# Second attention with the values as weights and its output as features by tokens; a router with fewer and reordered steps

## The reference

```python
p = jax.nn.softmax(s, -1).astype(v.dtype)
p_nb = p[..., :kh * kw].reshape(B, H, GRID_W, kh, kw)
p_ctx = p[..., kh * kw:]
return (jnp.einsum('bqhij,biqjhd->bqhd', p_nb, v_nb)
        + jnp.einsum('bqhp,bphd->bqhd', p_ctx, v_ctx))
```

```python
g_sel = jnp.argmax(g_logits, -1)
e_in_group = jnp.take_along_axis(e_logits, g_sel[:, None, None], 1)[:, 0]
top_v, top_i = lax.top_k(e_in_group, TOP_K)
gates = jax.nn.softmax(top_v, -1) * p_g
```

## Time and profile before

| | us |
|---|---|
| median of three timed runs (lowest, highest) | 1438.0 (1436.76, 1440.14) |
| profiled execution, its own time | 1435.37 |
| its span | 1433.2 |
| TensorE busy / VectorE / ScalarE / GpSimd | 1091.2 / 382.4 / 183.3 / 244.7 |
| weights of the experts, six pieces of 1 MB each | 246 pieces |
| DMA, mean over the span | 272 GB/s |

### The profile page before, as it was taken

The page is one execution under the profiler, slowest core; times in us unless marked ns, Lnnn a source line. Parts: engine busy times, 40 slices in busy tenths (PEclk is TensorE's granted clock), DMA queues, the critical chain, the costliest instruction groups (busy, mean ns, idle before and its releaser), DMA issues.

```text
span 1433.2 us, 26875 instructions
## 1 busy us (share of the span) xinstructions
PE 1091.2 (76%) x9881; PEld 586.6 (41%) x9882; DVE 382.4 (27%) x917; ACT 183.3 (13%) x486; POOL 244.7 (17%) x446
## 2 busy tenths in 40 slices
PE   4899998697587777656648999999935757788781
PEld 1333345444244444323224444677433423444440
DVE  0120117767311111101043002322772101111117
ACT  0110026300000000000012001542000000000000
POOL 2000002200133333212112010000001212333330
PEclk9999997997599999978787999898957978999996
DMA  9866891118959999999975992101079999999932
GB/s 367 293 242 257 341 364 57 59 60 309 414 212 395 415 416 414 415 416 415 397 287 87 110 165 101 59 1 59 30 274 413 412 414 416 415 366 370 416 111 112
DMA packets 84900, 389.72 MB, mean 272 GB/s; under 512 B 17613, under 2 KB 18125, under 8 KB 56697
## 3 DMA queue, kind: packets, MB, share of 16 engines
q1 hardware_dynamic: 62624, 349.77, 63.0%
q0 software_dynamic: 15200, 36.74, 9.2%
q10 hardware_dynamic: 7032, 2.66, 0.7%
HBM read 379.65 MB, written 17.44 MB: 277 GB/s over the span
## 4 chain that ended last, share of the span: by engine, by line
DMA 40%; PE 35%; issue 10%; DVE 9%; ACT 2%; DVEq 1%; POOLq 1%; POOL 0%; SPq 0%; ACTq 0%; PEldq 0%
DMA ring<-in_w_down_dram 32%; PE ps L800 15%; PE ps L951 6%; DMA ybuf<-yo,idy 4%; PE ps L1040 4%; DMA ring<-in_w_ada_dram 2%; PE ps L1058 2%; PE ps L921 2%; PE ps L776 1%; PE ps L888 1%; DMA ring<-in_w_gate_dram 1%; PE ps L895 1%; POOLq L450 1%; PE ps L906 1%; DMA qkv<-ybuf 1%
## 5 line engine op out<-in xcount | busy, mean ns | idle before, releaser
L1040 PE MATMUL ps<-ring,xs 128*32 128x256 f32 x4928 | 311.1, 406 | 112.7 <-DMA ring<-in_w_up_dram 59.1
L1040 PEld LDWEIGHTS ps<-ring,xs 128*32 128x32 f32 x4928 | 183.8, 116 | 234.0 <-issue 126.2
L800 PE MATMUL ps<-ring,hT 128*128 128x512 f32 x576 | 256.3, 604 | 8.1 <-ACT hT L626 4.3
L1058 PE MATMUL ps<-ring,hm 128*32 128x256 f32 x2464 | 156.5, 394 | 32.0 <-ACT hm L734 26.0
L800 PEld LDWEIGHTS ps<-ring,hT 128*128 128x128 f32 x576 | 110.1, 193 | 153.4 <-issue 143.0
L1058 PEld LDWEIGHTS ps<-ring,hm 128*32 128x32 f32 x2464 | 72.8, 112 | 91.7 <-ACT hm L734 39.9
L1507 DVE COPY yo<-ps 128x256 f32<-128x256 f32 x73 | 31.0, 425 | 237.2 <-DMA ybuf<-yo,idy 179.6
L539 POOL DMA_INDIRECT xg<-xmod,idx x77 | 80.8, 1050 | 66.3 <-POOL idx L536 61.4
L731 ACT ACTIVATE sg<-ps 128x128 f32<-128x128 f32 x73 | 20.3, 278 | 560.0 <-PE ps L1040 553.2
L951 PE MATMUL ps<-ring,qT 128*128 128x512 f32 x192 | 84.7, 601 | 2.7 <-DVE qT L1309 1.6
L550 POOL DMA_INDIRECT ybuf<-yo,idy x73 | 75.1, 1029 | 64.4 <-POOL idy L547 62.6
(11 more groups left out here) (257 smaller groups left out, 853.0 us busy)
## 6 DMA issues: line engine op xcount, KB each, us to landing
ring<-in_w_gate_dram SPq DMA_DIRECT2D x82, 1024.0 KB
ring<-in_w_up_dram SPq DMA_DIRECT2D x82, 1024.0 KB
ring<-in_w_down_dram SPq DMA_DIRECT2D x82, 1024.0 KB
ring<-in_w_ada_dram SPq DMA_DIRECT2D x48, 1024.0 KB, 8.1
ring<-in_w_qkv_a_dram SPq DMA_DIRECT2D x12, 1024.0 KB, 5.2
ring<-in_w_qkv_b_dram SPq DMA_DIRECT2D x12, 1024.0 KB, 15.4
modb<-mdram POOLq DMA_DIRECT2D x12, 512.0 KB, 7.1
qkv<-ybuf SPq DMA_DIRECT2D x6, 1024.0 KB, 8.3
```

Source lines behind the costliest of these rows:

```text
L800: ins = mm(ps[:, 2 * t + hf, :], lhs[:, k, t * P:(t + 1) * P], raw[:, slot, kk * D + hf * 512:kk * D + (hf + 1) * 512], start=(k == 0), st ...
L1040: ins = mm(ps[j * BLK:(j + 1) * BLK, 1, 0:W].rearrange("p (a n) -> p a n", a=2), xs[:, k, :], w[:, :, at:at + FW], start=(k == 0), stop=(k ...
L1058: ins = mm(ps[j * BLK:(j + 1) * BLK, 5, 0:WD], hm[:, 2 * c + q, :], ring[:, slot + GU + c, q * D + j * WD:q * D + (j + 1) * WD], start=(c ...
```

## The change

In the second attention VectorE divides the probabilities of a unit by their sums before they are turned (`normalise`), the values become the weights and the turned probabilities the moving operand, each head of a pair fills its half of the PSUM partitions, and VectorE copies a unit's output straight to `oT` (`take_oT`). The 24 transposes and three copies are gone, and `w_o` is loaded in another order of rows.

```diff
 def transpose_prob(u):
-    pe.wait_ge(comb_done[l] if l == 0 else exp_done[l], u + 1)
+    pe.wait_ge(comb_done[l], u + 1)
 def attend(u):
     pe.wait_ge(pT_ev[l], u + 1)
-    w = P // maps
-    for h in range(maps):
-        lo = j * P + h * w
-        for i in range(nk):
-            ins = mm(tile_ps(3)[:, lo:lo + w], probT[u % 2][:, h, i * P:(i + 1) * P], values(t, i, lo, lo + w),
-                     start=(i == 0), stop=(i == nk - 1))
+    ...
+    else:
+        if u >= 2:
+            pe.wait_ge(o_ev[l], u - 1)
+        for i in range(nk):
+            for h in range(2):
+                ins = mm(ps[HD * h:HD * (h + 1), 6 + u % 2, 0:P], values(t, i, lo + HD * h, lo + HD * (h + 1)),
+                         probT[u % 2][:, h, i * P:(i + 1) * P], start=(i == 0), stop=(i == nk - 1))
     ins.then_inc(pv_done[l], 1)
-transpose_tiles(lambda t: o[:, t, :], o_rdy[l], oT_ps[l])
-pe.wait_ge(oT_rdy[l], NT)
+if l == 0:
+    transpose_tiles(lambda t: o[:, t, :], o_rdy[l], oT_ps[l])
+    pe.wait_ge(oT_rdy[l], NT)
+else:
+    pe.wait_ge(o_ev[l], UNITS)
```

On VectorE, where layer 1 had `take_o` once in four units:

```diff
+def normalise(u):
+    t, j = u // PAIRS, u % PAIRS
+    e = prob[u % 2][:, :, 0:keys[t]]
+    r = rsum[:, 2 * (u % 2):2 * (u % 2) + 2]
+    dve.wait_ge(exp_done[l], u + 1)
+    chain(v.reciprocal(r, sums[:, t % 2, :, j]))
+    v.tensor_tensor(e, e, r.unsqueeze(2).to_broadcast([P, 2, keys[t]]), ALU.mult).then_inc(comb_done[l], 1)
+def take_oT(u):
+    t, j = u // PAIRS, u % PAIRS
+    dve.wait_ge(pv_done[l], u + 1)
+    v.tensor_copy(oT[:, j, t * P:(t + 1) * P], ps[:, 6 + u % 2, 0:P]).then_inc(o_ev[l], 1)
 ...
-        elif u >= 5 and u % 4 == 1:
-            take_o((u - 5) // 4)
+        else:
+            normalise(u)
+            if u >= 2:
+                take_oT(u - 2)
```

```diff
 # POOL, behind the writes of o
+last = x[:, NT - 1, :]
+chain(pool.tensor_tensor(last, last, lnb[:, 2, :], ALU.mult))
+pool.tensor_tensor(last, last, lnb[:, 3, :], ALU.add).then_inc(x2_done, 1)
 pool.wait_ge(mod_used, l + 1)
 load_gates(l, 1)
 ...
-pool.wait_ge(tok_rdy[l], 1)
-pool.wait_ge(tab_rdy[l], 1)
-n_blk = table(pool, T_NBLK, 24, NB)
 pool.wait_ge(xmod_w[l], 16 * NT)
 pool.wait_ge(out_done, 32 * (l + 1))
+pool.wait_ge(tok_rdy[l], 1)
 ...
 gather(0)
+pool.wait_ge(tab_rdy[l], 1)
+n_blk = table(pool, T_NBLK, 24, NB)
 # TensorE
+pe.wait_ge(rt_dve[l], 1)
+for t in range(NT):
+    ins = mm(ps[0:NE, 5, 0:1], a_all[:, t, :], ones[:, 0:1], start=(t == 0), stop=(t == NT - 1))
+ins.then_inc(rt_pe[l], 1)
 pe.wait_ge(key_rdy[l], 1)
 ... # the two key products
-pe.wait_ge(rt_dve[l], 2)
 ... # twelve products with tri and ones
-for t in range(NT):
-    ins = mm(ps[0:NE, 5, 0:1], a_all[:, t, :], ones[:, 0:1], start=(t == 0), stop=(t == NT - 1))
-ins.then_inc(rt_pe[l], 1)
 waves(6, 7)
 pe.wait_ge(rt_dve[l], 3)
 ...
-pe.wait_ge(rt_dve[l], 5)
 for i in range(2 * NT):
+    pe.wait_ge(rt_dve[l], 5 + i)
     ins = mm(ps[:, 1, 0:NBX], rt[:, 2400 + i * P:2400 + (i + 1) * P], ...)
 # VectorE, first_max (low is iota - 1000)
-chain(v.tensor_scalar(tmp, tmp, -1000.0, 1000.0, ALU.mult, ALU.add))
-chain(v.tensor_tensor(tmp, tmp, iota3(n), ALU.add))
+chain(v.scalar_tensor_tensor(tmp, tmp, -1000.0, iota3(n), ALU.mult, ALU.add))
 chain(v.tensor_reduce(col(20, NT), tmp, AX, ALU.min))
-chain(v.tensor_tensor(one, iota3(n), b3(col(20, NT), n), ALU.is_equal))
+chain(v.tensor_tensor(one, low, b3(col(20, NT), n), ALU.is_equal))
 # VectorE, other groups
-for t in range(NT):
-    chain(v.tensor_tensor(e4[:, t], e4[:, t], oneg[:, t, :].unsqueeze(2)..., ALU.mult))
-    chain(v.tensor_tensor(e4[:, t], e4[:, t], pen[:, t, :].unsqueeze(2)..., ALU.add))
+chain(v.tensor_tensor(e4, e4, pen.unsqueeze(3).to_broadcast([P, NT, NG, EPG]), ALU.add))
```

## The result

The changed kernel takes 1423.7 us (median, 1420.6 to 1427.0) beside 1439.1 for the kernel before on the same chip: ratio 0.9902, 95% interval 0.9885 to 0.9920, 14 us less. The forecast was 1412.5, range 1405 to 1421: right in sign, 11 us too fast, and the measured time lies outside the range. The profiled execution takes 1422.7 us (span 1420.6, against 1433.2 before): 12.6 less where the steps add up to 25.5.

The account below looks back on a forecast made before the run. Bounds: expert weight loads (layer 0 hanging on TensorE's first block, layer 1 on its stream's start), TensorE in the second attention, VectorE in the routers. -7.8 - 14.8 - 4.9 + 2.0 = -25.5 from 1438.0 gives 1412.5 us, range 1405 to 1421.

Parts of the forecast that it names:

- last tile's scaling on GpSimd: Both routers: the last tile's two norm-weight multiplications leave VectorE, 2.6 us less there; modb's loads go later in layer 1.
- The prediction's own sign of being wrong: A second-attention unit above 4 us, or a first block in layer 0 less than 6 us sooner.
- a_all is ready 4.8 us sooner: Layer 0's router: logits 2.55 us sooner and a chain 2.27 shorter, so a_all at 349.2 in place of 354.04.
- The first block is 7.8 sooner: Layer 0, attention output to first expert block: 6.0 + 1.1 + 0.7 us sooner, -7.8 (bounds -6 to -9.5).
- stream +2.0: Layer 1: modb's later loads enter the weight stream that bounds the stage, costing 2.0 us.
- as the loads in that stage hang on TensorE, all of it moves: Layer 0's experts: the whole gain at the first block, 7.8 us, reaches the end of the stage.
- a unit 3.27: Second attention: TensorE's unit falls from 3.86 to 3.27 us; its last attend comes 14.8 sooner (bounds -6 to -17).
- the ring: Second attention: oT copy, maxima, two exps, copy of transposed probabilities and hand-overs, 3.27 us from an attend to later transposes.
- oT, w_o and fold, -4.9: Behind the second attention: transposes and copies vanish, w_o starts 0.4 behind the last attend, 4.9 us saved.
- Clock drop: Rival, chance 0.22: TensorE's wait in the second attention's tail lowers its clock, slowing tail and w_o; 1418 us.
- Halves in series: Rival, chance 0.12: the attend's two 64-column halves don't run beside each other, the unit stays at 3.85; 1421 us.
- Stream helped: Rival, chance 0.09: GpSimd is quick, layer 1's stream starts with the picks and gains 2.6, not losing 2.0; 1408 us.

Follow-up runs that it names:

- e4: The changed kernel with the last tile's scaling back on VectorE, behind a_all and the keys, where it waits for TensorE: 1413.0 us, ratio 0.9835.
- e5: e4 plus two GpSimd operations of 128x1024 on a scratch tile that nothing reads, issued behind modb's loads: 1414.7 us, ratio 0.9849.
- e2: The kernel before with only the router's edits (trimmed chain, last tile's transposes in halves, its scaling on GpSimd): 1439.8 us, ratio 1.0024.
- e11: e8 with layer 1's ln_g and ln_b loads issued by SyncE once the last expert's weights have landed: 1408.9 us, ratio 0.9798.
- e8: e4 with VectorE taking a unit's maxima ahead of the oT copy in the second attention: 1411.6 us, ratio 0.9824.
- e9: e4 without the position bias products in the second attention: 1405.4 us, ratio 0.9778.
- e7: e4 with the second attention's attend issued head by head in place of in turn: 1416.9 us, ratio 0.9869.

## Why the prediction was right or wrong

**The step that failed is the last tile's scaling on GpSimd.** It was put down as 1.23 to 2.5 us an operation (it took 2.37), as free for VectorE, and as +2.0 through modb's loads. With it out of the way (e4) the whole is 9.6 us faster by the ratios. The prediction's own sign of being wrong, a first block in layer 0 less than 6 us sooner, came up: its first product is 4.1 sooner. What the step did:
- In both layers it holds up VectorE's router chain. Layer 0, "a_all is ready 4.8 us sooner": 1.9 sooner with it, 5.1 without (e4). "The first block is 7.8 sooner": by the cut, the first product is 4.3 sooner with it, 8.7 without. Cost in layer 0 at GpSimd's first copy: 4.0 us (33.6 behind the cut against 29.6); with modb's loads issued first 3.6 (e5). The Trainium skill has the rule that I missed (SBUF — State Buffer, Who interferes with whom): VectorE's scalar operations in a two-port mode, and those with two inputs in SBUF against a GpSimd operation that reads SBUF, share a port pair with GpSimd, and whichever comes second waits for the whole of the other's instruction; a reduction never does. The traces agree: TENSOR_SCALAR (2.55, 1.99) and SCALAR_TENSOR_TENSOR (1.79 in e5, 2.28 in e2) wait, and the four TENSOR_REDUCE that fall beside one of GpSimd's operations in the changed kernel and e2 take their usual 0.14 to 0.17. Which mode a scalar operation ran in no trace shows, and GpSimd stayed out for far longer than one instruction of VectorE (6.84 us). I had cited the rule on how slow GpSimd is (the Trainium skill, GPSIMD Engine Reference, Performance versus the Vector engine: 1.96 times VectorE's time; here 2.37 against 1.23, 1.93 times) and not the one on its being in the way.
- In layer 1, "stream +2.0": 6.1. The second operation began 1.72 late, the picks came 1.4 later in place of 2.6 sooner, so both modb's loads and the weights were late: 4.5 by bytes, 4.7 at the last long wait for weights. The other 1.4 have no shown cause. The forecast's bounds were too narrow as well: its own starts for the loads, 1050.6 and 1053.1 against 1049.80, are 0.8 to 3.3 later and not 0.7 to 2.9, and by the cut they were 4.3 later. e4, with the picks 2.6 sooner and modb's loads 2.1 sooner, has layer 1 as before (346.3): the 2.1 MB of modb then fill the time up to the weights at some 300 GB/s, and bytes taken out of it help (layer 1 in e11 is 2.5 us less than in e4, 3.2 less than in e8). "All else that the router saves there is hidden behind the stream" held.

**Layer 0, "as the loads in that stage hang on TensorE, all of it moves".** Counted from the cut, of 4.3 at the first product 2.4 arrive at the end; in e4 6.4 of 8.7. The fifth expert's load, which waits for TensorE, is issued 3.3 sooner (430.00 before, 426.72 after); from there the DMA engines are full (share 1.02 in each window of 50 us from 430 to 580), and the last load is issued 2.3 sooner. Where that last 1.0 went I can't tell from scatter, which is 3.7 us in this stretch for one and the same code. The inner steps held: group 5.7 behind a_all (5.8), products 2.8, toki 1.9 behind them, GpSimd 0.2 behind toki (0.3).

**Second attention, "a unit 3.27", -14.8.** From the end of the projections (891.4, 889.05) to the last attend it is 11.5 shorter. TensorE's unit was mis-sized: 3.86 less 0.58 leaves out that attend takes 0.80, not 0.70, and that transposes and the bias's last instruction each grew 0.05 to 0.1 beside it. The thirteen intervals from unit 8 to unit 21 take 45.6 in place of 42.9, 2.7 of the 3.3 us missing; the start up to unit 8 and the tail (7.8, not 7.5) have 0.3 each. That both bounds came out at 3.3 was chance: the ring is 3.02 (e9). The wait behind normalise cost nothing.

**oT, w_o and fold, -4.9:** right in each part: w_o 0.39 behind the last attend, the norm 16.5 behind (16.15), tile 2 at 43.3 (43.3).

**The rivals.** Clock drop: TensorE stands still 1.70 us at 969.64, and the granted clock stays 1.00 there (windows 969.6 to 970.6 and 973 to 974), where 2.25 us before 978 were followed by a fall. Halves in series: refuted by the unit of 3.51 and the attend of 0.80; in e7, which issues them in series, even that order takes less than the forecast's 1.28. Stream helped: its premise failed. None was the true case, engines in each other's way; I had looked for waits by semaphore only. That e4 comes out at the forecast is partly luck: its middle is 4 us short of it, layer 0 1 short and layer 1 2 better, and by stretches it saves 21.8 and not 25.5.

## What to carry to other kernels

Before an operation moves to GpSimd "in parallel", list what VectorE runs beside it: a chain of 0.2 us operations waited here for nearly the whole of a 2.4 us one, twice, and GpSimd stood idle beside the chain. Look first for a gap on the engine that has the work (5 us of waiting for TensorE here), and count which loads the helper issues behind it. Where a stage is bound by a stream, only bytes ahead of it and its start count; a load taken out of its way needs a place where no other load waits behind it.

## What the runs showed of the hardware

- GpSimd: a two-input 128x1024 fp32 operation takes 2.37 us (VectorE 1.23); with all operands one tile 1.91.
- A small VectorE operation can last until GpSimd's two-input operation ends, with no tile shared: 2.39 and 1.79 us in e5, where the same forms take 0.22 and 0.26 alone.
- Between its two operations GpSimd stands idle as "issue", with nothing in the profile to name: 0.73 (e2), 1.72 and 2.57 us, and 6.84 in e5. That it waits for VectorE's chain is inferred; the same code gave 0.73 in one execution and 2.57 in another.
- A VectorE record can start up to 0.7 us ahead of the GpSimd record that it waits for (1030.37 and 1031.06 in e5): the ends tell, not the starts.
- The block behind a wait of over 3 us for weights ran at either clock level, 1.93 or 3.64 us for the same 32 instructions (granted clock 1.00 before, 0.50 after), and the layer's end did not follow it.
- Twelve products of 64 columns of weights by 128 columns take 0.80 us when issued in turn to the two halves of the array, 1.08 half by half (e7).
